# Expert blocks of two MoE stages: shared copy of gathered rows, one instruction each for the rows' high and low parts, gather issued ahead of the scatter

## The reference, cut to what matters

```python
def body(acc, xs):
    rows, rw, e = xs
    xb = hpad[rows]
    y = (jax.nn.silu(xb @ we_gate[e]) * (xb @ we_up[e])) @ we_down[e]
    return acc.at[rows].add(y * rw[:, None].astype(y.dtype)), None
```

## Time and profile before

| | us |
|---|---|
| median of 3 runs (lowest, highest) | 3131.33 (3129.58, 3132.32) |
| the profiled execution | 3128.74 |
| its span | 3127.0 |
| TensorE busy | 2696.8 (86%) |
| VectorE busy | 1746.7 (56%) |
| ScalarE busy | 1241.8 (40%) |
| GpSimd busy | 1042.4 (33%) |

### The profile page before, as it was taken

The page is one execution under the profiler, slowest core; times in us unless marked ns, Lnnn a source line. Parts: engine busy times, 40 slices in busy tenths (PEclk is TensorE's granted clock), DMA queues, the critical chain, the costliest instruction groups (busy, mean ns, idle before and its releaser), DMA issues. The chain is left out here.

```text
span 3127.0 us, 39919 instructions
## 1 busy us (share of the span) xinstructions
PE 2696.8 (86%) x12102; PEld 1960.0 (63%) x12103; DVE 1746.7 (56%) x2591; ACT 1241.8 (40%) x1753; POOL 1042.4 (33%) x1119
## 2 busy tenths in 40 slices
PE   5999989787679999999999939958968999965997
PEld 2455446574267877777777737745745666754776
DVE  3767767654266678677786624545462111445663
ACT  2320124520055567566665623236122111215653
POOL 0860022124444445454453421384120000105432
PEclk8999975797789999999999979979989999977999
DMA  6430010323268789899898655000202111326972
GB/s 247 148 138 1 27 54 1 139 81 131 85 230 283 241 282 318 268 311 312 268 343 253 206 159 171 7 28 2 43 14 61 41 41 42 148 115 214 311 231 46
DMA packets 162929, 472.13 MB, mean 151 GB/s; under 512 B 38637, under 2 KB 67937, under 8 KB 142073
## 3 DMA queue, kind: packets, MB, share of 16 engines
q1 hardware_dynamic: 116576, 358.25, 30.5%
q0 software_dynamic: 44704, 108.22, 15.1%
q10 hardware_dynamic: 1544, 4.33, 0.3%
HBM read 419.82 MB, written 95.81 MB: 165 GB/s over the span
## 5 line engine op out<-in xcount | busy, mean ns | idle before, releaser
L1830 PE MATMUL psum<-moe_high,moe_xg_high 128*128 128x512 f32 x960 | 390.6, 407 | 21.8 <-DVE moe_xg_low L1925 11.8
L1832 PE MATMUL psum<-moe_high,moe_xg_low 128*128 128x512 f32 x960 | 378.7, 394 | 0.0
L1831 PE MATMUL psum<-moe_low,moe_xg_high 128*128 128x512 f32 x960 | 376.1, 392 | 0.0
L1920 DVE TENSOR_TENSOR moe_low<-moe_raw,moe_high 128x2048 fp32r<-128x2048 f32 x160 | 359.2, 2286 | 13.1 <-ACT moe_high L1865 12.9
L1865 ACT ACTIVATE moe_high<-moe_raw 128x2048 fp32r<-128x2048 f32 x160 | 297.8, 1917 | 0.2 <-DMA moe_raw<-in_w_e_up 0.2
L1817 PE MATMUL psum<-moe_high_down,moe_hid_high 128*128 x488 | 204.4, 419 | 41.7 <-DVE moe_hid_low L1935 41.6
L1830 PEld LDWEIGHTS psum<-moe_high,moe_xg_high 128*128 128x128 f32 x960 | 182.1, 190 | 59.2 <-issue 24.8
L1832 PEld LDWEIGHTS psum<-moe_high,moe_xg_low 128*128 128x128 f32 x960 | 181.3, 189 | 43.1
L1831 PEld LDWEIGHTS psum<-moe_low,moe_xg_high 128*128 128x128 f32 x960 | 182.2, 190 | 36.1
L1877 ACT ACTIVATE moe_y_blk<-psum,row_w 128x1024 f32 x124 | 138.0, 1113 | 143.9 <-PE psum L1819 143.9
L1761 POOL DMA_INDIRECT moe_second<-moe_y_blk,moe_is_now x48 | 120.8, 2517 | 219.5 <-ACT moe_y_blk L1877 215.5
(11 more groups left out here) (599 smaller groups left out, 5625.1 us busy)
## 6 DMA issues: line engine op xcount, KB each, us to landing
moe_raw<-in_we_gate SPq DMA_DIRECT2D x64, 1024.0 KB
moe_raw<-in_we_up SPq DMA_DIRECT2D x64, 1024.0 KB
moe_raw<-in_we_down SPq DMA_DIRECT2D x64, 1024.0 KB
x<-in_w_ada POOLq DMA_DIRECT2D x16, 1024.0 KB
moe_raw<-in_w_e_gate SPq DMA_DIRECT2D x16, 1024.0 KB
moe_raw<-in_w_e_up SPq DMA_DIRECT2D x16, 1024.0 KB
moe_raw<-in_w_e_down SPq DMA_DIRECT2D x16, 1024.0 KB, 8.6
w_ring<-in_w_in SPq DMA_DIRECT2D x12, 1024.0 KB, 8.6
```

Of the source, the lines that this page charges most:

```text
L1830: pe.matmul(to, x_hi, R(of_k(w_hi, k)), start=(k == 0), stop=False)
L1831: pe.matmul(to, x_hi, R(of_k(w_lo, k)), start=False, stop=False)
L1832: last = pe.matmul(to, x_lo, R(of_k(w_hi, k)), start=False, stop=(k == KD - 1))
L1920: dve.tensor_tensor(R(low[:, at:at + 2048]), raw[r][:, part], hi, ALU.subtract).then_inc(w_low, 1)
```

## The change

The copy of the landed rows is divided: VectorE takes the first 512 elements of every row, ScalarE the last 512, with a semaphore each. TensorE's turn and POOL's gather wait for both. ScalarE's copy stands at the end of its pass, behind take(g+1). The high part and the low part of the rows become one instruction of 1024 elements each, over both PSUM banks, and the turn signals once, behind its eighth transpose, where it signalled behind the fourth and the eighth. On POOL, gather(g+3) and landed now come ahead of scatter(g). At the start of a stage ScalarE's half of the first copy stands ahead of its first weight cut.

```diff
-        bgu, bh, bx = s.bank[0], s.bank[2], s.bank[4:6]
+        bgu, bh, bx = s.bank[0], s.bank[2], s.psum[:, 4 * 512:6 * 512]
+        HALF = D // 2
...
                     for q in range(2):
                         g = 2 * j + q
-                        scatter(g, q, g + 1, j + 1 + q)
-                        pool.wait_ge(moved, g + 2)
+                        pool.wait_ge(moved_v, g + 2)
+                        pool.wait_ge(moved_a, g + 2)
                         gather(g + 3, 1 - q)
                         landed(q, j + 2)
+                        scatter(g, q, g + 1, j + 1 + q)
                         free_y(1 - q, j + 1 + q)
...
                 def turn():
                     for k in range(KD):
-                        last = pe.transpose(bx[k // 4][:, (k % 4) * P:(k % 4 + 1) * P], xg[:, k * P:(k + 1) * P], s.ident[:, :])
-                        if k % 4 == 3:
-                            last.then_inc(turned, 1)
+                        last = pe.transpose(bx[:, k * P:(k + 1) * P], xg[:, k * P:(k + 1) * P], s.ident[:, :])
+                    last.then_inc(turned, 1)
...
-                def take(g, i):
-                    act.wait_ge(turned, 2 * g + i + 1)
-                    act.activation(R(xg_high[:, 4 * i:4 * i + 4, :]), bx[i].rearrange("p (k n) -> p k n", k=4), ACT.Copy).then_inc(xh_ready, 1)
+                def place(g):
+
+                    act.wait_ge(rows_in, g + 1)
+                    act.wait_ge(turned, g)
+                    act.activation(xg[:, HALF:D], landing[:, bass.ds((g & 1) * D + HALF, HALF)], ACT.Copy).then_inc(moved_a, 1)
+
+                def take(g):
+                    act.wait_ge(turned, g + 1)
+                    act.activation(R(xg_high[:, :, :]), bx.rearrange("p (k n) -> p k n", k=KD), ACT.Copy).then_inc(xh_ready, 1)
...
                     act.activation(silu[:, :], bgu[:, 0:F], ACT.Silu).then_inc(silu_ready, 1)
-                    take(g + 1, 0)
-                    take(g + 1, 1)
+                    take(g + 1)
+                    place(g + 2)
...
+                act.wait_ge(rows_in, 1)
+                act.activation(xg[:, HALF:D], landing[:, HALF:D], ACT.Copy).then_inc(moved_a, 1)
                 cut(0, 0, 0)
-                take(0, 0)
-                take(0, 1)
+                take(0)
+                place(1)
...
-                def take(g, i):
-                    dve.wait_ge(xh_ready, 2 * g + i + 1)
-                    k = slice(4 * i, 4 * i + 4)
-                    dve.tensor_tensor(R(xg_low[:, k, :]), bx[i].rearrange("p (k n) -> p k n", k=4), xg_high[:, k, :], ALU.subtract).then_inc(xl_ready, 1)
+                def take(g):
+                    dve.wait_ge(xh_ready, g + 1)
+                    dve.tensor_tensor(R(xg_low[:, :, :]), bx.rearrange("p (k n) -> p k n", k=KD), xg_high[:, :, :], ALU.subtract).then_inc(xl_ready, 1)
...
-                    dve.tensor_copy(xg[:, :], landing[:, bass.ds((g & 1) * D, D)]).then_inc(moved, 1)
+                    dve.tensor_copy(xg[:, 0:HALF], landing[:, bass.ds((g & 1) * D, HALF)]).then_inc(moved_v, 1)
```

More of the change, by code:

```diff
@@ L1694, in stage_experts @@
         gathered, added = ([sem(s, f"{name}_{n}{q}") for q in range(2)] for n in ("gathered", "added"))
-        rows_in, moved, y_free = (sem(s, f"{name}_{n}") for n in ("rows_in", "rows_moved", "y_free"))
+        rows_in, moved_v, moved_a, y_free = (sem(s, f"{name}_{n}") for n in ("rows_in", "rows_moved_v", "rows_moved_a", "y_free"))
         turned, xh_ready, xl_ready = (sem(s, f"{name}_{x}") for x in ("turned", "xh_ready", "xl_ready"))
@@ L1774, in _ @@
                 free_y(0, 1)
-                pool.wait_ge(moved, 1)
+                pool.wait_ge(moved_v, 1)
+                pool.wait_ge(moved_a, 1)
                 gather(2, 0)
@@ L1824, in one @@
                     r = pe.snap(slot_before, min_val=0, max_val=RAW - 1)
-                    pe.wait_ge(xh_ready, 2 * (g + 1))
-                    pe.wait_ge(xl_ready, 2 * (g + 1))
+                    pe.wait_ge(xh_ready, g + 1)
+                    pe.wait_ge(xl_ready, g + 1)
                     to = bgu.rearrange("p (u f) -> p u f", u=2)
@@ L1833, in one @@
                     last.then_inc(gu_done, 1)
-                    pe.wait_ge(moved, g + 2)
+                    pe.wait_ge(moved_v, g + 2)
+                    pe.wait_ge(moved_a, g + 2)
                     turn()
@@ L1852, in _ @@
                 pe.reg_mov(slot_before, 0)
-                pe.wait_ge(moved, 1)
+                pe.wait_ge(moved_v, 1)
+                pe.wait_ge(moved_a, 1)
                 turn()
@@ L1920, in cut @@
                         dve.tensor_tensor(R(low[:, at:at + 2048]), raw[r][:, part], hi, ALU.subtract).then_inc(w_low, 1)
-                def take(g, i):
-                    dve.wait_ge(xh_ready, 2 * g + i + 1)
-                    k = slice(4 * i, 4 * i + 4)
-                    dve.tensor_tensor(R(xg_low[:, k, :]), bx[i].rearrange("p (k n) -> p k n", k=4), xg_high[:, k, :], ALU.subtract).then_inc(xl_ready, 1)
+                def take(g):
+                    dve.wait_ge(xh_ready, g + 1)
+                    dve.tensor_tensor(R(xg_low[:, :, :]), bx.rearrange("p (k n) -> p k n", k=KD), xg_high[:, :, :], ALU.subtract).then_inc(xl_ready, 1)
                 def place(g):
                     dve.wait_ge(rows_in, g + 1)
-                    dve.wait_ge(turned, 2 * g)
-                    dve.tensor_copy(xg[:, :], landing[:, bass.ds((g & 1) * D, D)]).then_inc(moved, 1)
+                    dve.wait_ge(turned, g)
+                    dve.tensor_copy(xg[:, 0:HALF], landing[:, bass.ds((g & 1) * D, HALF)]).then_inc(moved_v, 1)
                 def take_hidden(g):
@@ L1956, in _ @@
                 dve.wait_ge(rows_in, 1)
-                dve.tensor_copy(xg[:, :], landing[:, 0:D]).then_inc(moved, 1)
+                dve.tensor_copy(xg[:, 0:HALF], landing[:, 0:HALF]).then_inc(moved_v, 1)
                 cut(0, 0)
-                take(0, 0)
-                take(0, 1)
+                take(0)
                 place(1)
```

## The result

The changed kernel takes 3159.73 us (median of 4 runs, 3156.83 to 3161.71); the kernel before took 3131.82 beside it (4 runs, 3129.58 to 3137.09). The ratio is 1.0086, 95% interval 1.0071 to 1.0101: slower, by 27.9 us between the medians. The forecast was 3163 in a range of 3137 to 3183. The two profiled executions lie further apart than the medians, 32.7 us by their spans: the one before is faster than every timed run of its kernel, the one after is the slowest of its four. Keep that in mind where rows of the table are subtracted.

What follows compares the result with a forecast made beforehand. The prediction took down's late start, behind ScalarE's and then VectorE's weight cut in boundary blocks, as the bound. Stage one +26.1, stage two +4.8, stage starts +3.6 and clock -3.1 made +31.4 on 3131.33: 3163 us, range 3137 to 3183.

Steps and rivals of the forecast that it cites:

- The chain that bounds: Boundary block: turn, ScalarE's high part, its first weight cut, VectorE's cut, its hidden low part, down at T + 10.85, 0.69 late.
- The sizes of the step: Boundary block: high part 1.11 us, half copy 0.61, VectorE's cut 0.98 later, down at T + 11.83, 1.67 late.
- Both delays count: Boundary block: the merged high part and ScalarE's half copy both delay the weight cut, VectorE's cut starting 0.98 late.
- The rival that only one counts: Boundary block: ScalarE's cut is only 0.5 late, down 1.19 late; total +6, 3137; chance 0.12.
- The count of 42 and 11: Boundary blocks whose late down costs time, from halved run lengths rounded up: 42 in stage one, 11 in stage two.
- Stage one and two: Late downs: stage one 70.1 against 44.0 now, +26.1; stage two 18.4 against 13.6, +4.8.
- Stage starts: Start of each stage: ScalarE's half copy waits for rows ahead of the weight cut, rows' low part 1.8 later; +3.6 in all.
- The clock: Two downs behind waits over 2 us ran mostly at 1.2 GHz; these slow stretches go, -2 x 1.57 = -3.1.
- POOL at nothing: POOL's gather, now under VectorE's weight cut, would be held up, but its new order is taken to cost 0.
- POOL's pace as the rival: Runs of boundary blocks: POOL takes about 10.7 a pass against the chain's 10.2; +24 less what is hidden, about 3183; chance 0.12.
- the sum of 31.4: Whole kernel: 26.1 for stage one, 4.8 for stage two, 3.6 for stage starts, -3.1 for the clock.
- faster: rows in time win: Boundary blocks: ScalarE's cut keeps its place, VectorE's cut starts at T + 3.57 everywhere; -20.5, 3111; chance 0.08.

Runs made afterwards that it cites:

- two halves: Changed kernel with turn signals behind the fourth and eighth transposes again, rows' high and low parts as two 512-element instructions each: 1.0034 of the kernel before.
- the cut first: Changed kernel with ScalarE's half of the first copy behind its first weight cut at each stage start: 1.0080 of the kernel before.
- the gather first: Kernel before with only gather and landed put ahead of the scatter on POOL: 0.9914 of the kernel before, 0.9930 when run again.
- small cuts: Kernel before with gather ahead of scatter and the weights' first two 2048-element pieces cut as four of 1024: 0.9886 of the kernel before, then 0.9890.
- VectorE copying all: Changed kernel with VectorE copying all 1024 elements and ScalarE none: 0.9962 of the kernel before.
- shared halves with small cuts: Changed kernel with two 512-element instructions for rows' high and low parts and the weights' first two pieces cut as four of 1024: 0.9924 of the kernel before.
- the scatter first: Changed kernel with POOL's scatter put back ahead of gather and landed: 1.0314 of the kernel before.

## Why the prediction was right, step by step

**The chain that bounds.** Right. Every edit that moved ScalarE's first cut in the boundary blocks moved VectorE's cut and down with it.

**The sizes of the step.** The rows' high part as one instruction takes 1.02, not 1.11, so the cut started at T + 2.51 and not 2.59, and down at T + 11.73 and not 11.83: 1.57 late, not 1.67. The half copy took 0.62 (forecast 0.61), VectorE's low part 1.22 (1.22). Gate and up was on time at T + 3.79 in these blocks.

**Both delays count.** Right, each shown by itself: going back to two halves gave 19 us, taking the copy off ScalarE some 40 us. The rival that only one counts is out.

**The count of 42 and 11.** Right in the sum, though the waits are 45 and 12. By waits down lost 55.3 + 45 x 0.25 = 66.6 in stage one, and 42 x 1.57 is 65.9; stage two has 15.3 + 12 x 0.25 = 18.3 against 11 x 1.57 = 17.3.

**Stage one and two.** Forecast, with a stage start and a vanished slow down in each: 26.1 + 1.8 - 1.6 = 26.3 and 4.8 + 1.8 - 1.6 = 5.0. Measured 24.6 and 3.3. The size that was off is the high part's 0.1 us, 5 over 53 blocks. With the measured waits stage one comes to 22.6 (down) + 0.8 (gate and up) + 1.7 - 1.6 = 23.5 of the 24.6, and stage two to 4.7 + 1.0 - 1.6 = 4.1 where 3.3 was measured.

**Stage starts.** From first to second turn +1.7 and +1.0, forecast 1.8 each. Stage two's start answers to the earlier trace rows:

```profile
2874.42 0.63 ACT L1913 ACTIVATE moe_xg<-moe_landing 128x512 f32<-128x512 f32 x1 [11.33 <-POOLq L1747]
2874.95 3.69 ACT L1869 ACTIVATE moe_high<-moe_raw 128x2048 fp32r<-128x2048 f32 x2
...
2876.88 4.49 DVE L1932 TENSOR_TENSOR moe_low<-moe_raw,moe_high 128x2048 fp32r<-128x2048 f32 x2 [2.10 <-ACT moe_high L1869]
...
2883.49 1.22 DVE L1936 TENSOR_TENSOR moe_xg_low<-psum,moe_xg_high 128x1024 fp32r<-128x1024 f32 x1
```

VectorE waits 2.10 for the first high part, as the step said. The kernel with the cut first won it back.

**The clock.** Right in the time: the two slow downs of the earlier trace rows have no answer after. The waits for down in the stages are at most 1.4 us long, but for the last of each, and none has slow matmuls behind it but the last of stage one (below). One reading was wrong: before, four waits of down are longer than 2 us and not two. The last downs of the stages, at 1825.53 and 3110.35, also waited 2.05, and ran at a granted clock of 1.00.

**POOL at nothing.** Right for the time, and right that its gather would be held (next section). POOL's pace as the rival is out: the kernel with the gather first has the same order on POOL and is 0.8% faster than before.

**What I did not have.** The stretch between the stages took 4.3 us longer in the trace, with the same code. All of it falls ahead of the first matmul behind stage one: from the last turn to there it is 49.0 before and 53.5 after, and from there on 977.5 and 977.3. Two things make it up. The last down of stage one waits 2.05 us in all thirteen traces; it ran at the low clock in five, both of the changed kernel among them, and took 1.6 longer there. And one VectorE instruction took 4.05 us after and 1.28 before:

```profile
1867.13 1.28 DVE L2610 SCALAR_TENSOR_TENSOR v_tok<-x,entry_sums,ssm_ES 128x1024 f32<-128x1024 f32 x1 [0.32 <-ACT entry_sums L2537]
```

```profile
1893.75 4.05 DVE L2619 SCALAR_TENSOR_TENSOR v_tok<-x,entry_sums,ssm_ES 128x1024 f32<-128x1024 f32 x1 [0.33 <-ACT entry_sums L2546]
...
1894.03 2.68 POOL L2517 TENSOR_TENSOR x<-x,v_tok 128x1024 f32<-128x1024 f32 x1
```

An addition on POOL starts 0.28 behind it here, and 0.93 behind it before. In the eight traces where that distance is 0.41 or less the instruction took 3.8 to 4.2, in the five where it is 0.51 or more 1.28 or 1.29. Neither is a property of the shared copy alone. The kernel with the gather first had the low clock in its second trace and not in its first, and the one with small cuts had the long instruction in its first and not in its second. All six traces with a shared copy have the long one, though; whether the change makes it likelier, the runs leave open.

So the sum of 31.4 is near the 32.7 between the two spans by luck: the stages were overestimated by 3.4, and the stretch between them, for which the sum has no term, put back 4.3. Between the medians 27.9 were measured, and the sum is 3.5 too high.

**The rival "faster: rows in time win".** It had about the right price for rows in time: alone they gave 27.9 and 21.6 us in two groups, and 21.0 for the two stages with 3.1 for the clock makes 24.1. The gain is in the result, and the shared copy and the merged instructions took more than all of it. It gave a ScalarE cut less than 0.39 late as the point of decision. The kernels on either side are in line with it: two halves is 0.52 late and 0.3% slower than before, and VectorE copying all is 0.38 late and 0.4% faster. The second gained more than the sum's terms give it, 53 x 1.07 = 56.7 against 57.6 and the 3.1 of the clock, some 4 us; it gained 11.8. In its trace gate and up's idle time in stage one is 5.2 us, where it was 9.1 before: that is the term the sum left out.

## What to carry to other kernels

Before dividing work between two engines, look which of them feeds the other at that place. Here VectorE waited for ScalarE, so relieving VectorE (0.26 us) was worth nothing, and each 0.1 us put in front of ScalarE's weight cut came out at the end. Merging two instructions removes a fixed cost of under 0.1 us, but also the overlap with the producer, which was worth 0.38 us here; cutting a first piece smaller, so that the consumer can start, was worth more than the fixed costs it added (0.5% of the time). Undo a change part by part: of three edits one was a gain of 0.8% and two were losses. And before a small difference of two traces is given to a change, look in which stretch it lies and whether two traces of one kernel differ as much there: here 4.2 us between the stages did.

## What the runs showed of the hardware

The issue of the gather, an indirect DMA of POOL, took 1.07 us on average before and 2.11 after, because it now falls under VectorE's weight cut, and its end follows the end of a piece of that cut. In the timeline above it starts at 1004.29, the first piece of the cut ends at 1003.82 + 2.29 = 1006.11, and the gather ends at 1007.06, 0.94 behind. It is 0.91 to 0.96, and mostly 0.94, for every gather that starts inside a piece in the changed kernel (80 in each of its two traces), in gather first (77), in small cuts (75) and in shared halves with small cuts (79). With the scatter first, where only 2 gathers start inside a piece, the mean is 1.08. With pieces of 1024 the issue takes 1.17, as above. In the two-halves kernel 31 of 80 are held so. The other 49 start at most 0.05 us behind the piece and take 1.07, like this one, whose piece starts at 1020.36. There VectorE pays: 49 of its cuts' first two pieces took 4.55 to 4.57, the 31 others 4.48 to 4.50.

```profile
1020.40 1.07 POOL L1741 DMA_INDIRECT moe_landing<-moe_rows,moe_ig_now  x1 [0.87 <-POOL moe_ig_now L1738]
```

The Trainium skill, "SBUF — State Buffer", section "Who interferes with whom", says that a VectorE instruction with two SBUF inputs contends with a GpSimd instruction that reads SBUF. The traces agree, and here the issue of an indirect DMA is held too. It cost no time, since a gather is needed two blocks later: no copy inside the loop of stage one waited for rows.

The addition on POOL between the stages shows the other side. In all eight traces where it starts at most 0.41 us behind VectorE's instruction, VectorE's ends 1.09 us behind the end of the addition, which itself takes 2.67 or 2.68.
